# Two attentions with the negated maximum taken in one step, and grouped attention in another unit order

## The reference, cut to what matters

```python
def _block_attention(q, k, v, scale):
    ...
        sc = jnp.einsum('bqkgd,bskd->bkgqs', qi, k,
                        preferred_element_type=jnp.float32) * scale
        p = jax.nn.softmax(sc, axis=-1).astype(v.dtype)
        return jnp.einsum('bkgqs,bskd->bqkgd', p, v)
...
def _gqa_axial(h, w_qkv, g_qn, g_kn, w_o, row, col):
    ...
    q = _axial_rope(_rms(q, g_qn), row, col)
    k = _axial_rope(_rms(k, g_kn), row, col)
    o = _block_attention(q, k, v, HD ** -0.5)
```

## Time and profile before

| | us |
|---|---|
| median of 3 runs (lowest, highest) | 2402.73 (2401.96, 2403.64) |
| the profiled execution | 2399.06 |
| its span, first to last instruction | 2397.3 |
| PE busy in the span | 2181.4 (91%) |
| DVE, ACT, POOL busy | 1694.8 (71%), 1298.8 (54%), 719.0 (30%) |
| grouped attention, of the span | about 1082 to 1609 |

### The profile page before, as it was taken

The page is one execution under the profiler, slowest core; times in us unless marked ns, Lnnn a source line. Parts: engine busy times, 40 slices in busy tenths (PEclk is TensorE's granted clock), DMA queues, the critical chain, the costliest instruction groups (busy, mean ns, idle before and its releaser), DMA issues. The chain is left out here.

```text
span 2397.3 us, 31526 instructions
## 1 busy us (share of the span) xinstructions
PE 2181.4 (91%) x10404; PEld 1604.7 (67%) x10404; DVE 1694.8 (71%) x1916; ACT 1298.8 (54%) x1528; POOL 719.0 (30%) x622
## 2 busy tenths in 40 slices
PE   8899997969999999987899999949969999999993
PEld 5566665747777777756677777737856777777772
DVE  3566664578888888873777777744268888888883
ACT  3344443147777777753544444333117777777773
POOL 1233331011332243215444444420001332333222
PEclk9999999979999999998999999979979999999997
DMA  7000003759999999942111111053269999999983
GB/s 266 3 12 12 11 13 129 277 216 379 383 385 391 388 383 383 395 140 88 45 49 49 51 48 48 14 193 103 99 247 345 386 381 387 389 380 383 396 301 127
DMA packets 176091, 519.86 MB, mean 217 GB/s; under 512 B 13120, under 2 KB 56896, under 8 KB 174976
## 3 DMA queue, kind: packets, MB, share of 16 engines
q1 hardware_dynamic: 168832, 493.53, 54.5%
q0 software_dynamic: 7168, 25.17, 4.5%
HBM read 480.91 MB, written 37.75 MB: 216 GB/s over the span
## 5 line engine op out<-in xcount | busy, mean ns | idle before, releaser
L1844 DVE TENSOR_TENSOR m_w_lo<-s_raw,m_w_hi 128x2048 fp32r<-128x2048 f32 x384 | 865.8, 2288 | 143.1 <-ACT m_w_hi L1788 142.0
L1788 ACT ACTIVATE m_w_hi<-s_raw 128x2048 fp32r<-128x2048 f32 x384 | 730.6, 1915 | 175.3 <-PE m_ps_down L1891 77.7
L1759 POOL DMA_INDIRECT acc<-m_ye,m_row_scatter x32 | 47.0, 1470 | 685.1 <-ACT m_ye L1805 685.1
L1889 PE MATMUL m_ps_gate<-m_w_hi,m_xeT_hi 128*96 128x512 f32 x512 | 205.4, 401 | 3.8 <-DVE m_xeT_lo L1850 3.8
L1889 PE MATMUL m_ps_down<-m_w_hi,m_hidT_hi 128*96 128x512 f32 x512 | 202.6, 396 | 3.8 <-DVE m_hidT_lo L1850 3.8
L1889 PE MATMUL m_ps_up<-m_w_hi,m_xeT_hi 128*96 128x512 f32 x512 | 203.7, 398 | 0.0
L1891 PE MATMUL m_ps_gate<-m_w_hi,m_xeT_lo 128*96 128x512 f32 x512 | 203.3, 397 | 0.0
L1891 PE MATMUL m_ps_down<-m_w_hi,m_hidT_lo 128*96 128x512 f32 x512 | 203.0, 397 | 0.0
L1891 PE MATMUL m_ps_up<-m_w_hi,m_xeT_lo 128*96 128x512 f32 x512 | 202.1, 395 | 0.0
L1890 PE MATMUL m_ps_gate<-m_w_lo,m_xeT_hi 128*96 128x512 f32 x512 | 201.9, 394 | 0.0
L1890 PE MATMUL m_ps_down<-m_w_lo,m_hidT_hi 128*96 128x512 f32 x512 | 201.4, 393 | 0.0
(11 more groups left out here) (234 smaller groups left out, 4435.1 us busy)
## 6 DMA issues: line engine op xcount, KB each, us to landing
s_raw<-in_w_gate SPq DMA_DIRECT2D x128, 1024.0 KB, 8.0
s_raw<-in_w_up SPq DMA_DIRECT2D x128, 1024.0 KB, 7.7
s_raw<-in_w_down SPq DMA_DIRECT2D x128, 1024.0 KB, 8.1
s_raw<-in_w_qkv_b SPq DMA_DIRECT2D x16, 512.0 KB, 4.5
s_raw<-in_w_qkv_b SPq DMA_DIRECT2D x32, 256.0 KB, 5.6
s_raw<-in_w_o_b SPq DMA_DIRECT2D x1, 8192.0 KB, 24.4
acc<-o_x SPq DMA_DIRECT2D x12, 512.0 KB, 5.3
xn<-o_xn SPq DMA_DIRECT2D x12, 512.0 KB, 4.1
```

The source lines that it names most:

```text
L1759: pool.indirect_dma_start(out=io.acc, out_offset=bass.IndirectOffsetOnAxis(ap=row_scatter[:, :], axis=0), in_=ye[:, :], in_offset=None, co ...
L1788: act.activation(hi[:, split, :, :].rearrange("p k n -> p (k n)"), raw[:, slot, :], ACT.Copy).then_inc(hi_ready, 1)
L1844: dve.tensor_tensor(lo[:, split, :, :].rearrange("p k n -> p (k n)"), raw[:, slot, :], hi[:, split, :, :].rearrange("p k n -> p (k n)"), A ...
L1889: pe.matmul(out[:, cols], left_hi[:, k, :], hi[:, split, kk, cols], start=(k == 0), stop=False)
```

## The change

**Scale and maximum, in both attentions.** `dve_max` becomes one reduction that writes the negated maximum; L311 and its semaphore go. The scale that L275 and L311 applied is put into q instead: in latent attention by ACT's four copies of q (a `scale=` on copies that are there already) and, for the rotary part, by one multiplication of the table `rope_T` on DVE behind the first tile's norm, which waits until all four table loads have landed; in grouped attention by one POOL multiplication of the q gains.

**Order, in grouped attention alone.** PE computes the scores of unit u+2 right behind the transposes of unit u's probabilities instead of at the end (the scores of unit 2 in unit 1, those of unit 3 at unit 1's end), projects half of the tile, computes the values product, and projects the other half. ACT's exponentials run two units ahead instead of one. On DVE the maximum of unit u+2 follows the copy of unit u, `dve_out` stands ahead of `squared`, and in unit 0 the q/k remainder stands behind `squared` and `values_low`. The weight splits stay at the end of units 2 and 4.

```diff
@@ class Core @@
         for j in range(2):
             act.activation(self.probs[:, unit % 2, j, 0:nk * P], self.S[:, unit % 2, j, 0:nk * P], ACT.Exp,
-                           bias=self.negmax[:, unit % 2, j:j + 1], scale=self.scale,
+                           bias=self.negmax[:, unit % 2, j:j + 1],
...
         dve.wait_ge(self.scores_done, n + 1)
-        wait(dve, self.negmax_done, n)
-        dve.tensor_reduce(self.rowmax[:, unit % 2, :], self.S[:, unit % 2, :, 0:nk * P], AX.X,
-                          ALU.max).then_inc(self.rowmax_done, 1)
-        dve.wait_ge(self.rowmax_done, n + 1)
         wait(dve, self.exp_done, 2 * n - 2)
-        dve.tensor_scalar(self.negmax[:, unit % 2, :], self.rowmax[:, unit % 2, :], -self.scale, None,
-                          ALU.mult).then_inc(self.negmax_done, 1)
+        dve.tensor_reduce(self.negmax[:, unit % 2, :], self.S[:, unit % 2, :, 0:nk * P], AX.X,
+                          ALU.max, negate=True).then_inc(self.negmax_done, 1)
@@ mla_block: one of four q copies, the use of the table, the table @@
-                    last = act.activation(qT[0:DN, 2 * slot, 0:PROMPT], bank[0:DN, PROMPT:], ACT.Copy)
+                    last = act.activation(qT[0:DN, 2 * slot, 0:PROMPT], bank[0:DN, PROMPT:], ACT.Copy, scale=SCALE)
...
+                if isinstance(g, int) and g == 0 and p == 0:
+                    dve.wait_ge(rope_scaled, 1)
...
             norm.dve_tile(dve, 0)
+            dve.wait_ge(tables_landed, 64)
+            dve.tensor_scalar(rope_T[2 * DR:, :], rope_T[2 * DR:, :], SCALE, None, ALU.mult).then_inc(rope_scaled, 1)
             for i in range(TILES + 1):
@@ gqa_block: POOL @@
             pool.wait_ge(tables_landed, 48)
+            pool.tensor_scalar(gains[:, 0, :], gains[:, 0, :], HD ** -0.5, None, ALU.mult).then_inc(gain_scaled, 1)
+            pool.wait_ge(gain_scaled, 1)
@@ gqa_block: ACT @@
                     core.act_copy(act, n, unit)
-                    if unit == 0:
-                        core.act_exp(act, n + 1, 1)
-                        if not last:
-                            projected(g + 1, 1 - slot, 0)
-                        turned(g, slot, TILES - 1, core.proj)
-                        continue
-                    if not (last and unit == NU - 1):
-                        core.act_exp(act, n + 1, (unit + 1) % NU)
+                    if unit == 1:
+                        core.act_exp(act, n + 1, 2)
+                    elif unit and not (last and unit >= NU - 2):
+                        core.act_exp(act, n + 2, (unit + 2) % NU)
                     if not last:
                         projected(g + 1, 1 - slot, unit)
+                    if unit == 0:
+                        turned(g, slot, TILES - 1, core.proj)
+                    elif not last:
                         turned(g + 1, 1 - slot, unit - 1, core.proj)
+                    if unit == 1:
+                        core.act_exp(act, n + 2, 3)
                     if unit in (2, 4) and not (isinstance(g, int) and g >= GROUPS - 2):
                         split_high(g + 2, slot, unit // 4)
@@ gqa_block: DVE @@
                     core.dve_copy(dve, n, unit)
+                    if unit == 1:
+                        core.dve_max(dve, n + 1, 2)
+                    elif unit and not (last and unit >= NU - 2):
+                        core.dve_max(dve, n + 2, (unit + 2) % NU)
...
-                    if unit == 0:
-                        turned(g, slot, TILES - 1, core.proj)
+                    core.dve_out(dve, g, n, unit, first)
                     if not last:
                         squared(g * NU + NU + unit, unit)
                         values_low(g + 1, 1 - slot, unit)
-                        if unit:
-                            turned(g + 1, 1 - slot, unit - 1, core.proj)
-                    core.dve_out(dve, g, n, unit, first)
-                    if not (last and unit >= NU - 2):
-                        core.dve_max(dve, n + 2, (unit + 2) % NU)
+                    if unit == 0:
+                        turned(g, slot, TILES - 1, core.proj)
+                    elif not last:
+                        turned(g + 1, 1 - slot, unit - 1, core.proj)
+                    if unit == 1:
+                        core.dve_max(dve, n + 2, 3)
                     if unit in (2, 4) and not (isinstance(g, int) and g >= GROUPS - 2):
                         split_low(g + 2, slot, unit // 4)
@@ gqa_block: PE @@
+            def next_scores(g, slot, unit, last):
+                if unit < NU - 2:
+                    scores(g, slot, unit + 2)
+                elif not last:
+                    scores(g + 1, 1 - slot, unit + 2 - NU)
...
                     core.pe_turn(pe, n, unit, shared.ident[:, :])
+                    if unit == 1:
+                        scores(g, slot, 2)
+                    elif unit:
+                        next_scores(g, slot, unit, last)
                     if not last:
-                        project(g + 1, 1 - slot, unit)
+                        project(g + 1, 1 - slot, unit, 0)
+                    core.pe_pv(pe, n, unit, lambda t: V[:, slot, t, :], lambda t: V_lo[:, 1 - slot, t, :])
+                    if not last:
+                        project(g + 1, 1 - slot, unit, 1)
                     if unit == 0:
                         turn(g, TILES - 1, core.proj)
                     elif not last:
                         turn(g + 1, unit - 1, core.proj)
-                    core.pe_pv(pe, n, unit, lambda t: V[:, slot, t, :], lambda t: V_lo[:, 1 - slot, t, :])
-                    if unit < NU - 2:
-                        scores(g, slot, unit + 2)
-                    elif not last:
-                        scores(g + 1, 1 - slot, unit + 2 - NU)
+                    if unit == 1:
+                        scores(g, slot, 3)
```

More of the change, by code:

```diff
@@ L181, with __init__ @@
 class Core:
-    def __init__(self, s, dk, dv, scale, o_dram, probs, probsT, out, probsT_lo=None):
-        self.dk, self.dv, self.scale, self.o_dram = dk, dv, scale, o_dram
+    def __init__(self, s, dk, dv, o_dram, probs, probsT, out, probsT_lo=None):
+        self.dk, self.dv, self.o_dram = dk, dv, o_dram
         self.S = s.psum("scores", [P, 2, 2, SAMPLE])
@@ L196, in __init__ @@
         self.pv = self.T[0:dv, 1, 0:2, :]
-        self.rowmax = s.sb("rowmax", [P, 2, 2])
         self.negmax = s.sb("negmax", [P, 2, 2])
@@ L201, in __init__ @@
         self.scores_done = s.sem("scores_done")
-        self.rowmax_done = s.sem("rowmax_done")
         self.negmax_done = s.sem("negmax_done")
@@ L405, in mla_block @@
         c_raw = s.sb("c_raw", [P, 2, W_IN])
-        core = Core(s, DN + DR, DV, (DN + DR) ** -0.5, io.o_a,
+        core = Core(s, DN + DR, DV, io.o_a,
                     s.sb("probs", [P, 2, 2, SAMPLE]), s.sb("probsT_sb", [P, 2, 4, P]),
@@ L420, in mla_block @@
         tables_landed = s.sem("tables_landed")
-        half_ready = s.sem("half_ready")
+        half_ready, rope_scaled = s.sem("half_ready"), s.sem("rope_scaled")
         c_done, c_copied = s.sem("c_done"), s.sem("c_copied")
@@ L442, in mla_block @@
         ROPES = [1, 2, 2, 3, 4, 4]
+        SCALE = (DN + DR) ** -0.5
         block = stack.enter_context(nc.Block())
@@ L567, in piece @@
                 if p == 0:
-                    last = act.activation(qT[0:DN, 2 * slot, 0:PROMPT], bank[0:DN, PROMPT:], ACT.Copy)
+                    last = act.activation(qT[0:DN, 2 * slot, 0:PROMPT], bank[0:DN, PROMPT:], ACT.Copy, scale=SCALE)
                 if p == 1:
-                    act.activation(qT[0:DN, 2 * slot + 1, 0:PROMPT], bank[0:DN, 0:PROMPT], ACT.Copy)
+                    act.activation(qT[0:DN, 2 * slot + 1, 0:PROMPT], bank[0:DN, 0:PROMPT], ACT.Copy, scale=SCALE)
                     last = act.activation(V[:, slot, 0:PROMPT_TILES, :].rearrange("p t n -> p (t n)"),
@@ L573, in piece @@
                 if p in (3, 4):
-                    last = act.activation(qT[0:DN, 2 * slot + p - 3, PROMPT:N], bank[0:DN, :], ACT.Copy)
+                    last = act.activation(qT[0:DN, 2 * slot + p - 3, PROMPT:N], bank[0:DN, :], ACT.Copy, scale=SCALE)
                 if p == 5:
@@ L890, in gqa_block @@
         V = s.sb("V", [P, 2, TILES, HD], F32R)
-        core = Core(s, HD, HD, HD ** -0.5, io.o_b, probs, probsT, out, probsT_lo)
+        core = Core(s, HD, HD, io.o_b, probs, probsT, out, probsT_lo)
         first_turns = core.T[:, :, :, :].rearrange("p b k n -> p b (k n)")
@@ L900, in gqa_block @@
         x_turned, x_high, x_split = s.sem("x_turned"), s.sem("x_high"), s.sem("x_split")
-        tables_ready = s.sem("tables_ready")
+        tables_ready, gain_scaled = s.sem("tables_ready"), s.sem("gain_scaled")
         half_ready = s.sem("half_ready")
@@ L1061, in _ @@
                     core.act_exp(act, 0, 0)
+                    core.act_exp(act, 1, 1)
                 if i >= TILES:
@@ L1183, in _, with project @@
         def _(pe):
-            def project(g, slot, t):
```

(8 more changed lines are left out.)

## The result

The changed kernel takes **2482.99 us** (median of four runs, 2482.80 to 2486.29) against 2402.35 before, a ratio of 1.0339 (95% interval 1.0321 to 1.0356): 3.4% slower. The forecast was 2460, with 2428 to 2486 as its range. The profiled execution has a span of 2481.3 against 2397.3: 84.0 more.

The account below looks back on a forecast made before the run. PE was taken as the bound, busy 332.7 of 355.0 us in six groups. Terms 9 - 4 + 0.75 + 48.6 + 4.5 - 5.7 + 4 = +57 on the profiled 2399.06 gave 2456, 3.67 under the median, so 2460; range 2428 to 2486.

Parts of the forecast that it names:

- the rival of the clock: Six groups: PE's clock falls to half behind twelve waits of 2.65, costing 12 x 2.2 = 26, not 4; 2482, chance 0.13.
- the bounds of the terms: Whole kernel: the forecast's own span from its terms' bounds, 2440 to 2475, given 0.64.
- the rotary table at the start: Program start: DVE's scaling waits for the table load, delaying PE's first projection from 15.12 to about 23.6; +9.
- latent attention, from there to its end: Latent attention: removing L311, for which ACT waits 22.1 in 33 waits, saves PE 4, between -6 and 0.
- start of grouped attention: Before the first group: unit 1's exponentials now stand ahead of ACT's first split; +0.75, between 0 and 1.4.
- six groups, without the clock: Grouped attention's six groups with splits: new PE waits make a group 67.25 instead of 59.1, +8.1 each; +48.6.
- the clock in these: Six groups: an odd drop or two of PE's clock behind the waits of 2.65; +4, of 0 to 26.
- group 6, T0 to T5: Last group, without splits: 52.7 against 48.17 before, with 5.45 of waits; +4.5.
- the tail: After T5: the 8 MB load goes out 3.4 earlier and most of 2.7 comes back; -5.7, between -6 and -2.
- the walk: Grouped attention, unit by unit: waits of 2.1, 2.1, 1.05, 2.95, 1.0 and 3.65, together 12.85 a group.
- 2.65 is nearer to 1.8: Six groups: waits up to 1.8 left the clock at 1.00, one of 4.73 preceded 0.50, so +4 was taken.

Follow-up runs that it names:

- e2: Changed kernel with PE computing the first half projection of units 3 and 5 an extra time, for nothing, ahead of the real one; 2470.33 us.
- e1: Changed kernel with the weight splits moved behind the copy of units 3 and 5 (on DVE behind the rotation); 2439.93 us.
- e6: Changed kernel with the copies of transposed q and k put ahead of the projection's own copies on ACT and DVE; 2467.10 us.
- e3: Changed kernel with the rotary table's scaling moved from behind the first norm to behind the first tile's compressed norm; 2476.91 us.
- e4: Kernel before with only the negated maximum and the scale in q, grouped attention's order as before, table scaling as in e3; 2397.24 us.
- e7: Changed kernel with e1's split, e3's table, e5's values product, scores before transposed probabilities, q/k copies first in units 0 and 5, rotation before reciprocals; 2393.45 us.
- e5: Changed kernel with the values product behind the whole projection and the q/k transposes on PE, ACT and DVE keeping the new order; 2460.30 us.
- e8: e7 with DVE's weight split at the end of units 3 and 4, and unit 0's output ahead of the q/k remainder; 2388.82 us.

## Why the forecast came out as it did

The sign, the places and the mechanism of the waits were right, and the time lay 23 above the forecast, on the rival of the clock (2482, chance 0.13). The range holds it, by 3, only because it was stretched to that rival: the bounds of the terms, 2440 to 2475, which had 0.64, do not. The terms, as the two profiled executions have them:

| term | forecast | measured |
|---|---|---|
| the rotary table at the start | +9 | +8.3 (first projection 15.12 to 23.42) |
| latent attention, from there to its end | -4 | -2.8 (8.2 apart at the compression's end, 5.4 at its own) |
| start of grouped attention | +0.75 | -1.7 (5.7 apart at its first row, 4.1 at the first T0) |
| six groups, without the clock | +48.6 | +53 (68.0 against 59.1 a group) |
| the clock in these | +4 | +27 (72.5 against 68.0 a group) |
| group 6, T0 to T5 | +4.5 | +4.4 (52.5 against 48.2) |
| the tail | -5.7 | -4.8 (44.2 against 49.0 from T5 to the last product) |

- **Unit by unit the walk held.** Unit lengths without a fall of the clock are 9.24, 10.63, 12.06, 13.09, 9.93 and 13.08 (the last from e2): waits of 1.9 for the bank in unit 0 (2.1 forecast), 1.9 for the scores in unit 1 (2.1), 0.83 in unit 2 (1.05), 0.1 and 2.9 in unit 3 (0.3 and 2.65), 0.7 in unit 4 (1.0), 0.7 and 2.9 in unit 5 (1.0 and 2.65). e1 showed that the split makes the waits of 2.9, e6 that the remainder makes the others but that of unit 2, which stands behind ACT's exponentials and the maximum.
- **The sum of the six lengths**, 68.0, is 0.8 above the forecast's 67.25, but by two errors that nearly cancel. The waits add up to 11.9, 0.9 less than the 12.85: the two behind the split are 0.25 longer (it takes 3.15 here against 2.74 in the row used), all others shorter. The work between the waits is 56.1 and not 54.4. Of these 1.7, 1.0 was there before: the prediction took 59.1 - 54.4 = 4.7 for waits, but PE was idle for 355.00 - 332.73 = 22.3 in the six groups, 3.7 a group. The other 0.7 is new with the order; which step it lies in was not followed. Those 3.7 were also all that a better order could win on PE with its work as it was.
- **The mis-sized term is the clock.** The step that failed is the sentence that 2.65 is nearer to 1.8, and so "an odd drop or two". The two rows gave only a wait that left the clock alone and one that didn't, and nearness to one of them says nothing on a wait that lies between; at the 4.73 the clock had fallen 2.1 ahead of the wait's end (1585.58 against 1587.71). Measured: at 11 of 12 waits of 2.9 the clock fell to half, from 0.5 ahead of the wait's end to 1.5 behind it, and at 5 of 12 waits of 1.9 to 2.4; 16 falls in six groups. One costs 1.5 to 1.8 (14.63 against 13.09, 12.4 against 10.63), below the 2.2 of the rival, and their number is above its 12; that 27 came out against its 26 is the luck of two errors that cancel. e2 shows the cause: with the same waits' ends and PE busy, 12 of the 16 falls are gone.
- **The start** was right in its chain, each step within 0.2: the scaling 0.56, the norm 1.28, the copy 0.68, the transposes 1.94. That nothing is given back was not quite right: e3 shows 6.7 at the end of latent attention and 6.1 at that of the program.
- **Latent attention** gained 2.8 of 4 here, 2.2 in e4; the bound of 0 to 6 held. The row that the term was built on was misread: PE's wait of 0.40 at 217.84 is on the output (L338), and PE's waits of that kind are the same 1.6 in 4 before, here and in e4. What fell are PE's waits on the copy of the probabilities (7.4 to 6.3) and on POOL's scaling (2.8 to 2.3); the rest of the gain was not followed.
- **The first exponentials** cost nothing that can be seen: grouped attention's preparation is 1.7 shorter, not 0.75 longer. Between its first row and the first T0 the granted clock was 0.50 for 18 us before and for 14 here, which may be it; no run separates this.
- **The tail**: the load was issued at T5+0.2 (1647.62), as forecast, against T5+3.5 before, and PE's wait for the output buffer behind it is 2.29 instead of 4.73.

**Open:** why waits of about 2 were followed by half clock in 5 cases in the changed kernel and in 10 in e1, and never in the seven of up to 1.8 before. In the tail of the kernel before, waits of 2.59 that end at 1579.49 and 1599.91 were not followed by it, one that ends at 1605.41 was. In the six groups of the other runs it was 4 of 12 at waits of 1.9 to 2.4 in e2, 2 of 6 at waits of 1.9 to 2.0 in e7, none of 6 at waits of 1.8 to 2.2 in e5, 5 of 6 at waits of 2.7 to 2.8 in e5, and all 12 at waits of 3.9 to 4.6 in e6. No run separates what PE does ahead of such a wait from its length.

## What to carry to other kernels

Computing a stage earlier can help only an engine that waited for that stage; what the moved work had covered (here, the copies between a projection and the next one) is uncovered, so list for each moved block what it stood in front of, and price the chain behind it from the moment that can't move. A wait that an engine near its limit gets new is to be priced twice: its length, and the work behind it at half clock; when the rows leave the second open between 0 and 26, the forecast should carry the middle, not the kinder end. And an edit that removes an instruction may put its replacement behind a wait: one multiplication at the start cost 6 to 8, more than the 48 instructions removed from latent attention gave.

## What the hardware showed that was not expected

**The weight split on DVE got longer when POOL worked beside it.** The four instructions took 2.74 in the row, with POOL idle, and 2.73 in each of the twelve splits of e1's six groups, with POOL idle too. In e7 they ran beside POOL's scaling of the probabilities, in e8 beside its normalising. DVE of e1, then DVE and POOL of e7, then of e8:

```profile
1256.80 2.73 DVE L1093 SCALAR_TENSOR_TENSOR s_w_qkv_lo<-s_raw,s_g_attn_b,s_w_qkv_hi 128x512 fp32r<-128x512 f32 x4
```

```profile
1298.28 4.29 DVE L1101 SCALAR_TENSOR_TENSOR s_w_qkv_lo<-s_raw,s_g_attn_b,s_w_qkv_hi 128x512 fp32r<-128x512 f32 x4
1298.38 2.98 POOL L296 TENSOR_TENSOR s_raw<-s_raw,b_rinv 128x512 f32<-128x512 f32 x2 [3.92 <-DVE b_rinv L313]
```

```profile
1300.16 4.14 DVE L1101 SCALAR_TENSOR_TENSOR s_w_qkv_lo<-s_raw,s_g_attn_b,s_w_qkv_hi 128x512 fp32r<-128x512 f32 x4
...
1300.18 0.83 POOL L969 TENSOR_TENSOR b_normed<-s_raw 128x384 f32<-128x384 f32 x1
1301.09 1.35 POOL L974 TENSOR_TENSOR s_raw<-b_normed,b_tables 128x384 f32<-128x384 f32 x1
```

4.29 and 4.14 instead of 2.74, and POOL is longer as well: 2.98 where the same scaling took 2.04 with DVE elsewhere, 1.35 where the multiplication by the table took 1.02. The Trainium skill, "SBUF — State Buffer", in "Who interferes with whom", says that a DVE instruction with two inputs in SBUF contends with a GpSimd instruction that reads SBUF, through a read interface that they share. The split has two such inputs (the raw weights and the high part), and the trace agrees, by 1.3 to 1.6 a split in these rows and 0.7 in unit 5 of e7, where the scaling is narrow. The 3.15 of the changed kernel is the same in small: the first of the four takes 1.16 beside the end of POOL's multiplication by the table, the other three 0.74 each. Most of what e8 misses would follow from it: the rotation behind the split and the copy is late by 0.9 to 1.0 in units 4 and 5, less than the 1.3 to 1.4 by which the split is longer, and these two waits are 2 of the 2.5 by which a group (58.0) exceeds the 55.5 that were expected. No run with the split moved away from POOL's work in e8 tests this.

**A wait of 2.9 us was enough for half clock, 11 times of 12.** Of a projection's 24 matmuls the rows of one of its three lines, in the changed kernel, two from the half ahead of the wait that ends at 1193.05 and the four behind it:

```profile
1187.87 0.39 PE L1202 MATMUL b_ps_projected<-s_w_qkv_hi,b_xnT 128*128 128x512 f32 x1
1188.57 0.39 PE L1202 MATMUL b_ps_projected<-s_w_qkv_hi,b_xnT 128*128 128x512 f32 x1
...
1194.54 0.60 PE L1202 MATMUL b_ps_projected<-s_w_qkv_hi,b_xnT 128*128 128x512 f32 x1
1195.80 0.63 PE L1202 MATMUL b_ps_projected<-s_w_qkv_hi,b_xnT 128*128 128x512 f32 x1
1197.08 0.63 PE L1202 MATMUL b_ps_projected<-s_w_qkv_hi,b_xnT 128*128 128x512 f32 x1
1198.19 0.40 PE L1202 MATMUL b_ps_projected<-s_w_qkv_hi,b_xnT 128*128 128x512 f32 x1
```

Three matmuls lie between one row and the next: 0.70 us ahead of the wait, at full clock (2.4 GHz), 1.26 and 1.28 in the stretch of 0.50 (1.2 GHz). This stretch begins at 1194.55, 1.5 after the wait has ended, so PE works in all of it. The one that begins at 1286.71 has its first 0.46 in the wait, and its unit takes 14.41, where the ten others of this kind take 14.6.
